# Index products kept in PSUM: the relu is written back into its bank, and VectorE reads it there

## The reference

```
logits = einsum('bqhe,bse->bqhs', qi, ki)            # 8 index heads of 32 channels
score  = einsum('bqh,bqhs->bqs', wi, relu(logits))   # weighted sum over the heads
score  = where(causal, score, -inf);  idx = top_k(score, 256)
```

## Time and profile before

| | |
|---|---|
| Median of 3 runs | 2379.61 us (2375.83 to 2385.45) |
| Profiled execution | 2373.25 us |
| Its span | 2371.5 us |
| TensorE matmul busy | 2240.0 us (94%) |
| VectorE busy | 1378.0 us (58%) |
| ScalarE busy | 848.8 us (36%) |
| GpSimd busy | 1146.9 us (48%) |
| Mean granted TensorE clock | 0.959 |

### The profile page before, as it was taken

The page is one execution under the profiler, slowest core; times in us unless marked ns, Lnnn a source line. Parts: engine busy times, 40 slices in busy tenths (PEclk is TensorE's granted clock), DMA queues, the critical chain, the costliest instruction groups (busy, mean ns, idle before and its releaser), DMA issues.

```text
span 2371.5 us, 31721 instructions
## 1 busy us (share of the span) xinstructions
PE 2240.0 (94%) x10040; PEld 1836.8 (77%) x10040; DVE 1378.0 (58%) x2542; ACT 848.8 (36%) x1290; POOL 1146.9 (48%) x642
## 2 busy tenths in 40 slices
PE   4786698999999999999999999999999999999999
PEld 3575576788888877788888888878888887888887
DVE  7888889368888853263777752436777644211111
ACT  4433444432332334434422324363233244322321
POOL 3554522155554600045655645575565565655653
PEclk8888897899999988999999999999999999999999
DMA  5111101123333301023223233223332324333332
GB/s 178 54 54 62 41 5 63 36 89 98 101 94 98 98 18 45 10 86 101 89 98 100 96 98 98 89 90 97 98 98 94 95 88 140 97 93 99 97 97 90
DMA packets 58548, 199.96 MB, mean 84 GB/s; under 512 B 6704, under 2 KB 6960, under 8 KB 58416
## 3 DMA queue, kind: packets, MB, share of 16 engines
q1 hardware_dynamic: 58416, 198.22, 26.5%
HBM read 194.00 MB, written 4.19 MB: 84 GB/s over the span
## 4 chain that ended last, share of the span: by engine, by line
PE 81%; DVE 6%; issue 3%; ACT 1%; POOL 1%; DVEq 0%; ACTq 0%; POOLq 0%
PE psum L450 24%; PE psum L451 24%; PE psum L452 24%; PE psum L617 3%; PE psum L476 2%; PE psum L595 2%; PE psum L594 1%; DVE score L1389 1%; DVE small L1384 1%; DVE small L1232 0%; PE psum L533 0%; DVE small L1231 0%; DVE small L1230 0%; POOL w_buf L733 0%; DVE score L1374 0%
## 5 line engine op out<-in xcount | busy, mean ns | idle before, releaser
L733 POOL TENSOR_TENSOR w_buf<-raw,w_buf 128x1024 fp32r<-128x1024 f32 x336 | 814.8, 2426 | 784.2 <-ACT w_buf L909 784.0
L450 PE MATMUL psum<-hid_buf,w_buf 128*128 128x512 f32 x1344 | 526.0, 391 | 4.6 <-DVE hid_buf L1459 2.8
L909 ACT ACTIVATE w_buf<-raw 128x1024 fp32r<-128x1024 f32 x336 | 353.2, 1052 | 493.9 <-PE psum L452 484.5
L452 PE MATMUL psum<-hid_buf,w_buf 128*128 128x512 f32 x1344 | 523.8, 390 | 0.0
L451 PE MATMUL psum<-hid_buf,w_buf 128*128 128x512 f32 x1344 | 523.6, 390 | 0.0
L450 PE MATMUL psum<-h_buf,w_buf 128*128 128x512 f32 x1216 | 475.3, 391 | 1.4 <-POOL h_buf L841 1.4
L452 PE MATMUL psum<-h_buf,w_buf 128*128 128x512 f32 x1216 | 473.3, 389 | 0.0
L451 PE MATMUL psum<-h_buf,w_buf 128*128 128x512 f32 x1216 | 473.2, 389 | 0.0
L1534 DVE TENSOR_TENSOR xt<-xt,psum 128x512 f32 (+1 forms) x160 | 110.0, 688 | 356.6 <-PE psum L452 356.2
L1555 DVE SCALAR_TENSOR_TENSOR psum<-y_buf,wdw,psum 128x512 f32<-128x512 f32 x464 | 314.0, 748 | 0.0
L450 PEld LDWEIGHTS psum<-hid_buf,w_buf 128*128 128x128 f32 x1344 | 252.7, 188 | 58.6 <-DVE hid_buf L1459 3.3
(11 more groups left out here) (194 smaller groups left out, 2338.0 us busy)
## 6 DMA issues: line engine op xcount, KB each, us to landing
raw<-weights SPq DMA_DIRECT2D x352, 512.0 KB, 3.5
xt<-x_t SPq DMA_DIRECT2D x2, 2048.0 KB, 7.9
x_in<-x_t SPq DMA_DIRECT2D x12, 256.0 KB, 4.9
out_t<-xt SPq DMA_DIRECT2D x1, 2048.0 KB, 10.2
out_t<-xt SPq DMA_DIRECT2D x8, 256.0 KB, 2.1
b_tok<-x_t SPq DMA_DIRECT2D x4, 256.0 KB, 5.8
ws<-w_s SPq DMA_DIRECT2D x1, 512.0 KB, 4.3
gvb<-g_vb SPq DMA_DIRECT2D x1, 256.0 KB, 4.2
```

The costliest lines, as they stand in the source:

```text
L450: nc.tensor.matmul(acc, lhs_hi, rhs_hi, start=first, stop=False)
L452: return nc.tensor.matmul(acc, lhs_lo, rhs_hi, start=False, stop=last)
L733: nc.gpsimd.tensor_tensor(dst_lo, raw[:, raw_slot], dst_hi.bitcast(F32), ALU.subtract).then_inc(lo_up, 1)
L909: nc.scalar.activation(dst, raw[:, raw_slot], ACT.Copy).then_inc(hi_up, 1)
```

## The change

Product n waits until tile n - 2 has been accumulated, not only put through the relu. The relu writes into the bank it reads, without waiting for VectorE. VectorE reads the bank. The two waits of ScalarE on `z_proc` go, which kept `tmp` free of VectorE's use of it as scratch in `process_keys`. The number of instructions on each engine stays.

```
-                    pe.wait_ge(logit_relu, n - 1)
+                    pe.wait_ge(logit_used, n - 1)
                 nc.tensor.matmul(psum[:, 2 + n % 2, 0:c1 - c0], ...).then_inc(logit_up, 1)
...
             def relu(n):
                 t, h, c0, c1 = LOGIT_TILES[n]
-                if n in (LOGITS[2], LOGITS[4]):
-                    act.wait_ge(z_proc, t // 4 * 16 + 4)
                 act.wait_ge(logit_up, n + 1)
-                if n >= 2:
-                    act.wait_ge(logit_used, n - 1)
-                nc.scalar.activation(tmp[:, n % 2, 0:c1 - c0], psum[:, 2 + n % 2, 0:c1 - c0], ACT.Relu
+                nc.scalar.activation(psum[:, 2 + n % 2, 0:c1 - c0], psum[:, 2 + n % 2, 0:c1 - c0], ACT.Relu
                                      ).then_inc(logit_relu, 1)
...
                 dve.wait_ge(logit_relu, n + 1)
-                dst, src, w = score[t][:, c0:c1], tmp[:, n % 2, 0:c1 - c0], w_idx[t % 4][:, h:h + 1]
+                dst, src, w = score[t][:, c0:c1], psum[:, 2 + n % 2, 0:c1 - c0], w_idx[t % 4][:, h:h + 1]
```

## The result

The changed kernel took 2399.96 us in the median of its five runs, the kernel before 2379.61, also of five. The ratio is 1.0075, with a 95% interval of 1.0049 to 1.0100. The forecast of 2384 us was 16 us too low, its range of 2369 to 2397 did not hold the time, and rival (b), priced at 2402 us, is nearest to what happened. The profiled execution took 2392.67 us against 2373.25, 19.4 us more.

A forecast was written before the change was run, and what follows sets the result against it. TensorE is busy 94% of the span, but VectorE arrives last in most projection steps. Terms -1 - 1.4 + 4.8 + 2.5 = +4.9 us on 2373.25 give 2378; that execution lies 6.4 below the median, so 2384, range 2369 to 2397.

The forecast's parts named there:

- rival (b): Early stop paid, with slower clock, at the third product of ten of thirteen steps: +22.6 us, 2402; chance 0.12.
- the wait: Expected sign: TensorE's wait at the index product grows from 26.7 to 40 us or so, put down to VectorE.
- Steps 21 to 25: Projection stage: products moved behind VectorE's first tile cost 0 to +1.8 us by step 24, mostly swallowed; net -0.35.
- The half clock: TensorE at 1.2 GHz after new stops of steps 29 to 31: +2.5 us, bounds 0 and 5.
- steps 29 to 31: Four-tile steps, GpSimd idle: later products delay VectorE's normalisation by 1.9, 1.8 and 1.1 us, +4.8, clock apart.
- steps 6 and 8: Projection stage: step 6 gains 0.4 to 0.9 us, step 8 about 0.2; together -1 us.
- steps 25 to 28: -1.4 us: -1.05 from steps 26 and 27 plus -0.35 before them; step 28 at TensorE's pace.
- Mostly swallowed: Before step 26, GpSimd's last rotation, undisturbed by VectorE, gives back 2.2 us against a delay of up to 1.8.
- Steps 26 and 27: TensorE's pace of 0.92 to 1.03 us a tile replaces VectorE's 1.15: -1.05 us.
- The accumulation: VectorE's 512-column tile takes 691 ns with one operand in PSUM; 19.2 us of VectorE saved in all.
- The relu: ScalarE's relu from PSUM to PSUM: taken as unchanged from 0.599 us, 7 us more as the upper end.
- (a): Rival: VectorE freed of GpSimd contention is the only bound, all 19 us come off, 2360; chance 0.09.

The follow-up runs named there:

- e2: The changed kernel plus 6 to 24 throwaway TensorE matmuls (fills) ahead of the third index product of nine steps; ratio 1.0047.
- e6: The kernel before plus throwaway TensorE matmuls (fills) ahead of the fifth index product of steps 6, 8, 22, 23 and 24; ratio 0.9973.
- e4: The kernel before with the changed in-place form only for tiles 40 to 63 (steps 25 to 27); ratio 0.9994.
- e1: The kernel before with only the wait changed: product n waits for accumulation n-2, relu still goes to SBUF; ratio 1.0066.
- late places: The changed kernel with all but the first two index products of steps 6, 8, 21 to 24, 29 to 31 behind the step's projection products; ratio 0.9992.

## Why the prediction was wrong

**The mechanism and its place were right, and its price was put on the wrong steps.** Every step with a stop was named, and the wait was forecast at 40 us and measured at 40.8, though the forecast shows no working for the 40. The step that failed is "Steps 21 to 25: between 0 and +1.8 us at the end of step 24". The trace says +13.5 (+10.2 in the second), of which +3.0 came from step 8. I counted there only the order, two eighths of products at 0.23 us each. The half clock I put into step 6, at 0.5 to 1 us, and into steps 29 to 31, as a term of 2.5 us with an upper bound of 5. Steps 21 to 24 got none, although showed it after the stop of step 6, and although their new stops were longer than those of steps 29 to 31: 5.3 us in step 21, 5.1 in step 22, 4.2 in step 23, 7.9 in step 24. With fills in both kernels (e2 and e6) the same place in the table is at +4.0 us, +3.9 of it from steps 21 to 24. So the order was undersized there as well, by some 2 us or more, and the clock made up the rest. Over the whole stage the clock term measured 7 to 12 us instead of 2.5, and everything else 7.1 instead of 2.4.

By place, the 19.3 us are +3.0 in steps 6 and 8 (forecast -1), +10.4 in steps 21 to 24 (0 to +1.8), -2.9 in steps 25 to 28 (-1.4, with the delay before them set off) and +8.8 in steps 29 to 31 (+7.3). By the second traces of both kernels the four are +2.8, +6.4, -3.0 and +7.8.

**"Mostly swallowed".** GpSimd's last rotation did shrink as forecast, 298.48 to 302.91, 4.4 us, and TensorE got 1.8 of the 2.2 us back there: its last index product of step 25 was 13.2 us late, its first of step 26 11.4 (303.96 against 292.53). But what is given back is fixed, and it met a delay of 13 us, not 1.8. A slack swallows no more than its own size.

**Steps 6 and 8**, forecast -1, are +3.0. In step 6 the faster accumulations just paid for the slow restart (+0.5). In step 8, where GpSimd does not disturb VectorE, nothing was to be won.

**Steps 26 and 27**, forecast -1.05, gave -0.8 at TensorE from step to step: its first index product of step 26 is 11.4 us late, that of step 28 10.6. From the third product of step 26, where the forecast began to count, it is -1.8 (12.4 late, then 10.6); the difference is mostly the stop of 0.84 us at that third product, which the forecast left out. VectorE gains 4.5 us from step 25 to step 27 and loses 2 of them in step 28 again. TensorE's pace was 0.98 us a tile (306.85 to 321.21, between my 0.92 and 1.03).

**Steps 29 to 31**, forecast 4.8 by order and 2.5 by clock, 7.3 together, measured 8.8 (7.8 in the second trace): about right.

**The accumulation** was priced at 0.691 us by line 1596; it is 0.749. The line it came from has no scalar in an SBUF column as its operand; what makes the difference was not tried. Over the four forms this is 4.2 us of VectorE in the stage; how much of it is on the path was not measured. The relu, 0.584 against 0.599, was rightly taken as unchanged.

**Rivals.** (a), the freed port, is true as a mechanism (e4) and the PSUM form is worth 4 to 8 us here (e1 against the changed kernel), not 19. For (b) I gave 0.12; its text had the place, the price and the rule "it decides once six steps or so pay in full". What I held against it, that eight-tile steps are repaid by shorter accumulations, holds only where GpSimd disturbed them: steps 8, 23 and 24 had 0.75 us tiles before, too.

## What to carry to other kernels

When a buffer is dropped between two engines, the producer's queue stops earlier by exactly that buffer; list every place where the consumer comes late, and put the price of a stop on each of them, not on the ones looked at last. If one row of the trace shows TensorE at 1.2 GHz after a stop, every new stop of that length may have it too, on all products behind it, and the forecast needs the term or a range that holds it. Then take off what the kernel before pays already behind its own stops. Independent work in the stop, even matmuls whose result is thrown away, can pay: it took 12 to 16 us off the changed kernel's stage and 3.6 off that of the kernel before, and a third bank with it made the kernel 0.7% faster than the first one. Before crediting it to a change, give the kernel before the same remedy.

## What the runs showed of the hardware

- In the first trace of the changed kernel all seven stops of 3.13 to 7.9 us at an index product were followed by products recorded at 0.63 us instead of 0.39; the four of 0.63, 0.67, 0.84 and 1.63 us were not. The length of a stop does not decide alone: in the second trace the 3.13 us of step 29 had products at 0.40 us behind them, and in the kernel before a stop of 2.02 us (step 23) had six at 0.63. In the kernel with fills the longest stop was 2.5 us, and of ten one alone, of 1.99 us in step 8, had slow products behind it.
- VectorE's accumulation with one operand in PSUM took 751 ns at most in 70, also beside GpSimd; with two in SBUF it took up to 2498 ns, and above 0.76 us only beside GpSimd. Undisturbed, both forms take 0.75 us at 512 columns. The multiplication by a scalar, undisturbed, takes 0.49 us from SBUF and 0.75 from PSUM.
- Two traces of one kernel end the stage 4.3 us apart for the changed kernel, 2.7 for the one with late places, 1.1 for the kernel before, and 0.1 for the changed kernel with fills.
